# The MLP's up layers one to three as seven products of quarters, with parts of x streamed from DRAM

## The chip, the core and the metric

The kernel runs on one core of one Trainium2 chip. The metric is the device time of one execution, from the first to the last instruction and what lies around them. The core's engines run their own queues of instructions and meet at semaphores: TensorE (PE in the profile, its weight loads PEld), VectorE (DVE), ScalarE (ACT), GpSimd (POOL), and SyncE (SP), which issues transfers.

## What is computed

The kernel is two transformer blocks in a row on 512 tokens of width 1024. The change concerns only the last step of the second block, the MLP:

```python
D_FF = 4 * D_MODEL          # 4096, D_MODEL is 1024, 512 tokens
hm = rmsnorm(x, norm_mlp_g[l])
x = x + jnp.square(jax.nn.relu(hm @ w_up[l])) @ w_down[l]
...
return rmsnorm(x, norm_final_g)
```

## The kernel before

Products of float32 matrices are made from two halves of each operand: a high half, rounded to the format that TensorE takes, and a low half, the rest. `three_pass` (line 229) issues three matmuls, high by high, high by low, low by high. So each weight tile of 128x2048 numbers (1 MB, a "unit") is copied by ScalarE into its high half (`unit_high`, line 2843) and subtracted into its low half by GpSimd or VectorE (`unit_lower`, line 2851; `LOWERED_BY_VECTOR` says which are VectorE's). Units stand in rings of three, so the high half of one waits for the product three before it.

The MLP is cut into four layers of 1024 features. Layer zero's up product (`up0`) is a dense layer like the others in the kernel. In layers one to three an up product (`up`, line 3106) takes eight tiles of 128 features by 512 tokens, eight steps of 128 along the width each, so 64 times three matmuls of 512 columns, with four units. Its result leaves PSUM by `rectified` on VectorE, is squared on ScalarE, and is cut into parts for the down product.

The down product (`down`, line 3136) is already Strassen's in Winograd's form: the two matrices are cut into quarters, seven products of sums of quarters (`product`, line 3120) take the place of eight. The sums of the features are made by `sums` (line 3004) with low halves by `parts_low`, the sums of the weights by `weights_1` to `weights_4`; each product's result is added to the rows of x by `add` (line 3042) on VectorE. Products share PSUM banks: a later one accumulates on the result of an earlier one, and so it waits until that has been added (`p_added`).

Every engine's order is written out by hand in `mlp_sync`, `mlp_gpsimd`, `mlp_scalar`, `mlp_vector` and `mlp_tensor`. An engine stands still at an instruction whose semaphore isn't there yet, with all that is queued behind it.

## Time and profile before

| what | us |
|---|---|
| median of three runs | 1572.93 (1571.53 to 1573.01) |
| profiled execution, its span | 1574.5 |
| TensorE busy | 1550.3 |
| VectorE busy | 980.6 |
| ScalarE busy | 790.5 |
| GpSimd busy | 591.0 |
| the MLP's stages, from up0 to the last product | 1235.4 to 1568.1 of the span |

The profiled execution's own time is its span, with nothing beside it that the profile shows. Busy time of an engine is the time in which at least one of its instructions ran. Matmuls overlap their neighbours, so how long one keeps TensorE is read from the distance of starts. A wait is put down to the instruction that ended it.

### The profile page before, as it was taken

To read this page: it belongs to the slowest core of one execution; us is meant where nothing else is said; L and a number is where in the kernel's file an instruction comes from. 1 tells how busy PE (TensorE), PEld (TensorE's weight loads), DVE (VectorE), ACT (ScalarE), POOL (GpSimd) and SP (SyncE) were. 2 spreads that over 40 slices of the span, in tenths; PEclk is the share of its full clock that TensorE was granted. 3 is DMA by queue.
4 is the path that set the end of the run, shared out by engine and by line. 5 is a ranking of instruction groups with operands and counts; after the bars stand their busy time and mean duration, and the time that the engine had idled before them with its cause. 6 is when DMAs were issued, how large, how long until landed. Compare 5 with 4: busy or idle time off the path is not lost.

```text
span 1574.5 us, 20093 instructions
## 1 busy us (share of the span) xinstructions
PE 1550.3 (98%) x7516; PEld 1263.7 (80%) x7516; DVE 980.6 (62%) x1234; ACT 790.5 (50%) x926; POOL 591.0 (38%) x254
## 2 busy tenths in 40 slices
PE   9999999999999899999999999999999999999998
PEld 7888788687878788888889868767888888888886
DVE  6366211783465699999987479773454574656556
ACT  5265222435245588888875251695334353434344
POOL 1422354533442232232221746444332335252524
PEclk9999999999999999999999999999999999999999
DMA  5421242212237799999976314401420405050411
GB/s 206 128 74 54 80 148 95 106 54 107 82 111 294 276 420 413 386 389 385 390 276 254 116 67 142 131 1 54 160 81 27 161 27 187 28 187 27 171 57 54
DMA packets 50055, 252.18 MB, mean 160 GB/s; under 512 B 9984, under 2 KB 12800, under 8 KB 23744
## 3 DMA queue, kind: packets, MB, share of 16 engines
q1 hardware_dynamic: 43344, 237.89, 41.0%
q0 software_dynamic: 5184, 8.40, 1.5%
q10 hardware_dynamic: 1456, 4.92, 0.8%
q8 instruction: 47, 0.77, 0.2%
q14 instruction: 24, 0.20, 0.0%
HBM read 235.57 MB, written 16.78 MB: 160 GB/s over the span
## 4 chain that ended last, share of the span: by engine, by line
PE 84%; issue 5%; DVE 5%; DMA 2%; ACT 2%; POOL 2%; SPq 0%; ACTq 0%; DVEq 0%; POOLq 0%; PEldq 0%
PE psum L232 23%; PE psum L234 23%; PE psum L233 23%; POOL w_both L148 2%; PE psum L703 2%; PE psum L2402 2%; PE psum L2437 1%; PE psum L1080 1%; PE psum L2425 1%; PE psum L1373 1%; DMA moe_w<-in_w_moe 1%; PE psum L705 1%; PE psum L724 1%; PE psum L2726 1%; PE psum L1059 1%
## 5 line engine op out<-in xcount | busy, mean ns | idle before, releaser
L148 POOL TENSOR_TENSOR w_both<-raw,w_both 128x2048 fp32r<-128x2048 f32 x62 | 288.9, 4659 | 438.0 <-ACT w_both L142 403.1
L1391 DVE TENSOR_TENSOR moe_lo<-moe_w,moe_hi 128x2048 fp32r<-128x2048 f32 x100 | 228.0, 2291 | 35.7 <-ACT moe_hi L1381 34.8
L232 PE MATMUL psum<-x_hi,w_both 128*128 128x512 f32 (+1 forms) x624 | 241.8, 388 | 2.6 <-POOL w_both L148 2.6
L234 PE MATMUL psum<-x_hi,w_both 128*128 128x512 f32 (+1 forms) x624 | 239.5, 384 | 0.0
L233 PE MATMUL psum<-x_lo,w_both 128*128 128x512 f32 (+1 forms) x624 | 239.5, 384 | 0.0
L142 ACT ACTIVATE w_both<-raw 128x2048 fp32r<-128x2048 f32 x67 | 128.0, 1911 | 196.3 <-PE psum L234 194.3
L1381 ACT ACTIVATE moe_hi<-moe_w 128x2048 fp32r<-128x2048 f32 x100 | 191.3, 1915 | 34.3 <-PE psum L234 16.6
L2854 POOL TENSOR_TENSOR unit_lo<-mlp_raw,unit_hi 128x2048 fp32r<-128x2048 f32 x24 | 111.1, 4630 | 180.2 <-ACT unit_hi L2849 102.6
L232 PEld LDWEIGHTS psum<-x_hi,w_both 128*128 128x128 f32 x624 | 117.3, 188 | 27.7 <-issue 3.1
L233 PEld LDWEIGHTS psum<-x_lo,w_both 128*128 128x128 f32 x624 | 117.3, 188 | 23.2 <-issue 0.5
L234 PEld LDWEIGHTS psum<-x_hi,w_both 128*128 128x128 f32 x624 | 117.2, 188 | 23.3
L2849 ACT ACTIVATE unit_hi<-mlp_raw 128x2048 fp32r<-128x2048 f32 x40 | 76.3, 1914 | 77.1 <-PE psum L234 44.6
L232 PE MATMUL psum<-moe_hi,moe_xt_hi 128*128 128x512 f32 x256 | 100.6, 393 | 2.8 <-issue 1.6
L234 PE MATMUL psum<-moe_hi,moe_xt_lo 128*128 128x512 f32 x256 | 99.8, 390 | 0.0
L233 PE MATMUL psum<-moe_lo,moe_xt_hi 128*128 128x512 f32 x256 | 99.7, 389 | 0.0
L232 PE MATMUL psum<-unit_hi,f_hi 128*128 128x512 f32 x224 | 87.5, 391 | 0.9 <-DVE res_rows L3049 0.6
L232 PE MATMUL psum<-y_hi,w_both 128*128 128x512 f32 x224 | 87.8, 392 | 0.0
L234 PE MATMUL psum<-y_hi,w_both 128*128 128x512 f32 x224 | 87.2, 389 | 0.0
L234 PE MATMUL psum<-unit_hi,f_lo 128*128 128x512 f32 x224 | 87.2, 389 | 0.0
L233 PE MATMUL psum<-y_lo,w_both 128*128 128x512 f32 x224 | 87.2, 389 | 0.0
L233 PE MATMUL psum<-unit_lo,f_hi 128*128 128x512 f32 x224 | 87.1, 389 | 0.0
L232 PE MATMUL psum<-x_hi,unit_hi 128*128 128x512 f32 x192 | 74.7, 389 | 0.0
(438 smaller groups left out, 3358.2 us busy)
## 6 DMA issues: line engine op xcount, KB each, us to landing
raw<-in_w_dense SPq DMA_DIRECT2D x67, 1024.0 KB, 4.9
moe_w<-in_w_moe_ahead SPq DMA_DIRECT2D x54, 1024.0 KB, 13.2
moe_w<-in_w_moe SPq DMA_DIRECT2D x48, 1024.0 KB, 13.8
mlp_raw<-in_w_mlp SPq DMA_DIRECT2D x28, 1024.0 KB, 4.9
yrow<-expert_rows SPq DMA_DIRECT2D x8, 512.0 KB, 7.1
res<-in_x SPq DMA_DIRECT2D x4, 512.0 KB, 6.7
decay<-in_decay SPq DMA_DIRECT2D x8, 256.0 KB, 5.2
hn_rows<-hn_tok ACTq DMA_DIRECT2D x4, 512.0 KB, 6.3
```

The source lines that it names most:

```text
L142: act.activation(w_hi[c % RING][:, :], raw[c % RING][:, :], ACT.Copy).then_inc(hi_ready, 1)
L148: pool.tensor_tensor(w_lo[c % RING][:, :], raw[c % RING][:, :], w_hi[c % RING][:, :].bitcast(F32), ALU.subtract).then_inc(lo_ready, 1)
L232: pe.matmul(out, lh, rh, start=first, stop=False, **more)
L233: pe.matmul(out, lh, rl, start=False, stop=False, **more)
L234: return pe.matmul(out, ll, rh, start=False, stop=last, **more)
L703: pe.matmul(psum[:, bank, :], x_hi[:, kt, rows], wb[:, :, :, kt, :], start=kt == 0, stop=kt == KT - 1, skip_group_check=True)
L705: mm = pe.matmul(psum[:, bank, 0:2 * P], x_lo[:, kt, rows], wb[:, 0, :, kt, :], start=False, stop=kt == KT - 1, skip_group_check=True)
L1381: act.activation(ring_hi[s % MOE_HI][:, :], ring[s][:, :], ACT.Copy).then_inc(moe_high, 1)
L1391: dve.tensor_tensor(ring_lo[s][:, :], ring[s][:, :], ring_hi[s % MOE_HI][:, :].bitcast(F32), ALU.subtract).then_inc(moe_low, 1)
L2402: mm = pe.matmul(out, lhs, rhs, start=(qt != 0), stop=True, skip_group_check=True)
L2849: act.activation(unit_hi[(U + 2) % 3][:, :], unit_source(U)[:, :], ACT.Copy).then_inc(highs_done, 1)
L2854: eng.tensor_tensor(unit_lo[(U + 2) % 3][:, :], unit_source(U)[:, :], unit_hi[(U + 2) % 3][:, :].bitcast(F32), ALU.subtract).then_inc(lows ...
```

## The change

In layers one to three the up product becomes seven products too. The weights of the up layer come in quarters (512 of the width by 512 features), the quarters of x (512 of the width by 256 tokens) and their four sums are made once, with high and low halves, and written to DRAM (`x_parts`); each product loads its part back into a ring of three (`x_ring`). A product (`features`) is 48 matmuls of 256 columns. Four of the seven results accumulate in one pair of banks, others are copied by ScalarE (`copy_out`) and added by VectorE (`rectified_quad`), so that the four quarters Q11, Q12, Q22, Q21 of the features come out one after the other. Their sums and halves are now made quarter by quarter (`f_sums`, `part_high`, `part_low`). Up and down stages both have seven units; of an up stage's units VectorE lowers the third and the fifth, of a down stage's the first, GpSimd the others. The order of the down products changes to A11, A12, S1, S4, S2, S3, A22, and with it the order of the additions. Layer zero keeps its dense up product, with another order around it. The core of the diff, with the removed lines mostly left out:

```diff
-        add_residual(dve, "o_cross", norm_mlp)
+        add_residual(dve, "o_cross", norm_mlp, invert=False)
...
-    LOWERED_BY_VECTOR = (0, 2, 3, 5)
-    UNITS = PRODUCTS + 4
+    STAGES = 2 * G - 1
+    PART_OF_PRODUCT = (A11, A12, S1, S4, S2, S3, A22)
+    BANKS_X, BANKS_UP, BANKS_Y, BANKS_Z = (1, 2), (6, 7), (4, 5), (3, 0)
...
+    f_quads = at("f_quads", 112, [P, 2, 2, 4, MIDDLE])
+    Q11, Q12, Q22, Q21 = (1, 0), (1, 1), (0, 1), (0, 0)
+    x_quads = at("x_quads", 188, [P, 2, 2, 4, MIDDLE])
+    x_quads_lo = at("x_quads_lo", 188, [P, 2, 2, 4, MIDDLE], FR)
+    x_quads_hi = at("x_quads_hi", 144, [P, 2, 2, 4, MIDDLE], FR)
+    X_SUMS = ((2, Q22), (5, Q21), (4, Q11), (3, Q12))
+    x_parts = nc.dram_tensor("x_parts", [PRODUCTS, P, 2, 4, MIDDLE], F32).ap()
+    x_ring = [at(f"x_part{b}", 48 + 8 * b, [P, 2, 4, MIDDLE], FR) for b in range(3)]
+    first_s1 = at("first_product", 72, [P, 2, S])
+    c_relu = [at(f"c_relu{h}", 76 + 2 * h, [P, S]) for h in range(2)]
...
+    SUM_OF_UNIT = {2: 1, 4: 2, 5: 3, 6: 4}
+    RAW_OF_UNIT = (B11, B21, B11, B22, B11, B12, B21)
+    LOWERED_BY_VECTOR = ((0,), (2, 4))
...
+        def load_part(K):
+            if K < PRODUCTS * (G - 1):
+                g, n = divmod(K, PRODUCTS)
+                if K >= 3:
+                    before = divmod(K - 3, PRODUCTS)
+                    sp.wait_ge(p_done, 2 * PRODUCTS * (2 * before[0] + 1) + 2 * before[1] + 2)
+                sp.dma_start(x_ring[K % 3][:, :, :, :].bitcast(F32), x_parts[n]).then_inc(part_landed[K % 3], 16)
...
+            part(3)
+            part(4)
+            weights(B11, 3, 3)
+            part(5)
+            weights(B21, 4, 4)
+            part(6)
+            weights(B12, 5, 4)
+            part(7)
+            part(8)
+            weights(B22, 6, 4)
+            part(9)
...
+    def x_sum_low(eng, i, lowered):
+        q = X_SUMS[i][1]
+        eng.wait_ge(xs_high, CROSS + i + 1)
+        if i in (0, 2):
+            eng.wait_ge(xs_added, CROSS + (3, 0, 4)[i])
+        eng.tensor_tensor(quad(x_quads_lo, q), quad(x_quads, q), quad(x_quads_hi, q).bitcast(F32), ALU.subtract)\
+           .then_inc(lowered, 1)
...
+        x_sum_low(pool, 0, xs_low_pool)
+        x_sum_low(pool, 1, xs_low_pool)
...
+        def square(g, q):
+            for h in range(2):
+                act.wait_ge(c_relued, CROSS + quad_count(g, q, h))
+                act.activation(quad(f_quads, q, h), c_relu[h][:, :].rearrange("p (m n) -> p m n", n=MIDDLE), ACT.Square)\
+                   .then_inc(c_squared, 1)
+
+        def part_high(g, part, q):
+            for h in range(2):
+                if part in SUM_COUNT:
+                    act.wait_ge(f_summed, sums_count(g, SUM_COUNT[part]))
+                else:
+                    act.wait_ge(c_squared, SQUARED + quad_count(g, q, h))
+                act.activation(f_parts[h][:, :, 0, part, :], quad(f_quads, q, h), ACT.Copy).then_inc(f_high, 1)
+
+        def copy_out(g, n, h):
+            act.wait_ge(p_done, 2 * PRODUCTS * (2 * g - 1) + 2 * n + h + 1)
+            if n == 3:
+                act.wait_ge(c_squared, SQUARED + quad_count(g, Q11, h))
+            elif n == 1 and g > 1:
+                act.wait_ge(c_squared, SQUARED + quad_count(g - 1, Q21, h))
+            out = first_s1[:, h, :] if n == 2 else c_relu[h][:, :]
+            act.activation(out, psum[:, (BANKS_Z if n == 1 else BANKS_Y)[h], :], ACT.Copy).then_inc(s1_copied, 1)
...
+            up, down = PRODUCTS * (2 * g - 1), PRODUCTS * 2 * g
+            unit_high(act, up + 2)
+            unit_high(act, up + 3)
+            copy_out(g, 1, 0)
+            copy_out(g, 1, 1)
+            unit_high(act, up + 4)
+            copy_out(g, 2, 0)
+            square(g, Q11)
+            copy_out(g, 2, 1)
+            unit_high(act, up + 5)
+            copy_out(g, 3, 0)
+            part_high(g, A11, Q11)
+            copy_out(g, 3, 1)
+            unit_high(act, up + 6)
+            square(g, Q12)
+            unit_high(act, down)
+            part_high(g, A12, Q12)
+            square(g, Q22)
+            unit_high(act, down + 1)
+            part_high(g, A22, Q22)
+            unit_high(act, down + 2)
+            square(g, Q21)
+            part_high(g, S1, Q22)
+            unit_high(act, down + 3)
+            part_high(g, S4, Q12)
+            part_high(g, S2, Q11)
+            part_high(g, S3, Q21)
...
+    SUM_COUNT = {S1: 1, S3: 2, S2: 3, S4: 4}
+    ADDED_AFTER = {0: -13, 1: 0, 2: -9, 3: -10, 4: 3, 5: 2, 6: -8}
+    ADDED_TO = ((2, 0), (2, 0), (0, 1), (2, 1), (2, 1), (0, 1), (0, 0))
...
+        def f_sums(g):
+            q11, q12, q22, q21 = (quad(f_quads, q) for q in (Q11, Q12, Q22, Q21))
+            dve.wait_ge(c_squared, SQUARED + quad_count(g, Q21, 1))
+            dve.tensor_tensor(q22, q21, q22, ALU.add).then_inc(f_summed, 1)
+            dve.tensor_tensor(q21, q11, q21, ALU.subtract).then_inc(f_summed, 1)
+            dve.wait_ge(f_summed, sums_count(g, 1))
+            dve.tensor_tensor(q11, q22, q11, ALU.subtract).then_inc(f_summed, 1)
+            dve.wait_ge(f_summed, sums_count(g, 3))
+            dve.tensor_tensor(q12, q12, q11, ALU.subtract).then_inc(f_summed, 1)
+
+        def part_low(g, part, q):
+            for h in range(2):
+                dve.wait_ge(f_high, part_count(g, part, h))
+                dve.tensor_tensor(f_parts[h][:, :, 1, part, :], quad(f_quads, q, h),
+                                  f_parts[h][:, :, 0, part, :].bitcast(F32), ALU.subtract).then_inc(f_low, 1)
+
+        def rectified_quad(g, q, h):
+            first = 2 * PRODUCTS * (2 * g - 1)
+            n = {Q11: 1, Q12: 4, Q22: 5, Q21: 6}[q]
+            x = psum[:, BANKS_UP[h], :]
+            nth = quad_count(g, q, h)
+            dve.wait_ge(p_done, first + 2 * n + h + 1)
+            if q in (Q22, Q21):
+                dve.wait_ge(c_squared, SQUARED + nth - 2)
+            out = c_relu[h][:, :]
+            if q != Q21:
+                dve.wait_ge(s1_copied, copies_count(g, {Q11: 1, Q12: 3, Q22: 2}[q], h))
+                other = first_s1[:, h, :] if q == Q22 else out
+                dve.tensor_tensor(out, x, other, ALU.add).then_inc(c_read, 1)
+                dve.wait_ge(c_read, READ + 6 * (g - 1) + 2 * C_ORDER.index(q) + h + 1)
+            m = "p (m n) -> p m n"
+            rstd = norm_mlp.rstd[:, MIDDLE * q[0]:MIDDLE * (q[0] + 1)].unsqueeze(1).to_broadcast([P, 2, MIDDLE])
+            ins = dve.scalar_tensor_tensor(out=out.rearrange(m, n=MIDDLE), in0=(x if q == Q21 else out).rearrange(m, n=MIDDLE),
+                                           scalar=0.0, in1=rstd, op0=ALU.max, op1=ALU.mult)
+            ins.then_inc(c_relued, 1)
+
...
+        x_sums()
+        x_sum_low(dve, 2, xs_low_dve)
+        x_sum_low(dve, 3, xs_low_dve)
+        norm_mlp.vector_invert(dve)
         norm_mlp.wait_inverted(dve)
         dve.wait_ge(bank_free, UP0_T + 4)
+        for c in range(4):
+            rectified(2 * c)
+            rectified(2 * c + 1)
+            sums(c)
+            parts_low(c)
+            if c == 2:
+                unit_lower(dve, 0)
+                weights(0, 1)
+        dve.wait_ge(rows_read, ONCE + 2 * TB)
+        add(0, 0)
+        weights(0, 2)
+        weights(0, 3)
+        add(0, 1)
+        weights(0, 4)
+        add(0, 2)
+        add(0, 3)
+        add(0, 4)
+        add(0, 5)
+        for g in range(1, G):
+            up, down = 2 * g - 1, 2 * g
+            add(g - 1, 6)
+            weights(up, 1)
+            unit_lower(dve, PRODUCTS * up + 2)
+            weights(up, 2)
+            weights(up, 3)
+            rectified_quad(g, Q11, 0)
+            rectified_quad(g, Q11, 1)
+            weights(up, 4)
+            unit_lower(dve, PRODUCTS * up + 4)
+            part_low(g, A11, Q11)
+            rectified_quad(g, Q12, 0)
+            rectified_quad(g, Q12, 1)
+            unit_lower(dve, PRODUCTS * down)
+            rectified_quad(g, Q22, 0)
+            part_low(g, A12, Q12)
+            rectified_quad(g, Q22, 1)
+            weights(down, 1)
+            part_low(g, A22, Q22)
+            rectified_quad(g, Q21, 0)
+            rectified_quad(g, Q21, 1)
+            f_sums(g)
+            part_low(g, S1, Q22)
+            weights(down, 2)
+            part_low(g, S4, Q12)
+            add(g, 0)
+            weights(down, 3)
+            part_low(g, S2, Q11)
+            part_low(g, S3, Q21)
+            add(g, 1)
+            add(g, 2)
+            weights(down, 4)
+            add(g, 3)
+            add(g, 4)
+            add(g, 5)
...
+        def features(g, n):
+            L, K = 2 * g - 1, PRODUCTS * (g - 1) + n
+            wh, wl = unit(PRODUCTS * L + n)
+            pe.wait_ge(part_landed[K % 3], PARTS_LANDED[K % 3] + 16 * (K // 3 + 1))
+            x = x_ring[K % 3]
+            banks = (BANKS_UP, BANKS_Z, BANKS_Y, BANKS_Y, BANKS_UP, BANKS_UP, BANKS_UP)[n]
+            for h in range(2):
+                if n == 0 and g > 1:
+                    pe.wait_ge(c_relued, CROSS + quad_count(g - 1, Q21, h))
+                elif n < 3:
+                    pe.wait_ge(p_added, 2 * PRODUCTS * (g - 1) + 2 * (1, 1, 3)[n] + h + 1)
+                elif n == 3:
+                    pe.wait_ge(s1_copied, copies_count(g, 2, h))
+                else:
+                    pe.wait_ge(c_relued, CROSS + quad_count(g, C_ORDER[n - 4], h))
+                for m in (2 * h, 2 * h + 1):
+                    out = psum[:, banks[h], MIDDLE * (m % 2):MIDDLE * (m % 2 + 1)]
+                    for k in range(4):
+                        w = slice(m * P, (m + 1) * P)
+                        mm = three_pass(pe, out, wh[:, k, w], wl[:, k, w], x[:, 0, k, :], x[:, 1, k, :],
+                                        n < 3 and m % 2 == 0 and k == 0, k == 3, skip_group_check=True)
+                mm.then_inc(p_done, 1)
+
...
+        def product(g, n, pairs=range(4)):
+            wh, wl = unit(PRODUCTS * 2 * g + n)
+            f = PART_OF_PRODUCT[n]
             for i in range(2):
+                if n >= 3:
+                    pe.wait_ge(p_added, 2 * PRODUCTS * g + 2 * (2, 0, 4, 5)[n - 3] + i + 1)
+                elif n == 0 and g:
+                    pe.wait_ge(p_added, 2 * PRODUCTS * (g - 1) + 2 * 6 + i + 1)
                 rows = slice(i * P, (i + 1) * P)
                 for c in pairs:
```

## Rows read from the trace of the kernel before

**Rows 1.** The page, part 1: the span, and TensorE's busy time, share, instructions.

```profile
span 1574.5 us, 20093 instructions
PE 1550.3 (98%) x7516; PEld 1263.7 (80%) x7516; DVE 980.6 (62%) x1234; ACT 790.5 (50%) x926; POOL 591.0 (38%) x254
```

**Rows 2.** Busy time by window: layer one's up stage, then its down stage.

```profile
core 0: us, PE busy (x) PEld busy (x) DVE busy (x) ACT busy (x) POOL busy (x), PEclk, DMA share, GB/s
...
1322.40:1365.90 43.50, 43.50 (x193) 36.04 (x192) 20.56 (x25) 16.77 (x14) 13.58 (x4) 1.00 0.22 80
1365.90:1404.30 38.40, 38.31 (x169) 31.44 (x168) 26.98 (x25) 15.54 (x9) 18.76 (x5) 1.00 0.35 128
```

**Rows 3.** Waits of TensorE, 1235.4 to 1574: us in total, times, longest.

```profile
PE psum L232 <- DVE res_rows L3049: 0.6, 1, 0.6
```

**Rows 4.** Timeline of TensorE: first matmul of four stages (start us, us).

```profile
1283.43 0.39 PE L232 MATMUL psum<-unit_hi,f_hi 128*128 128x512 f32 x1
...
1322.39 0.39 PE L232 MATMUL psum<-x_hi,unit_hi 128*128 128x512 f32 x1
...
1365.91 0.39 PE L232 MATMUL psum<-unit_hi,f_hi 128*128 128x512 f32 x1
...
1404.35 0.39 PE L232 MATMUL psum<-x_hi,unit_hi 128*128 128x512 f32 x1
```

**Rows 5.** Timeline of TensorE: matmuls of 256 columns, 46 steps apart.

```profile
836.03 0.28 PE L233 MATMUL psum<-moe_lo,v_mem_in_hi 128*128 128x256 f32 x1
...
841.53 0.28 PE L234 MATMUL psum<-moe_hi,v_mem_in_lo 128*128 128x256 f32 x1
```

**Rows 6.** Timeline of GpSimd: three low halves.

```profile
1238.90 4.61 POOL L148 TENSOR_TENSOR w_both<-raw,w_both 128x2048 fp32r<-128x2048 f32 x1 [7.60 <-ACT w_both L142]
...
1262.41 6.41 POOL L148 TENSOR_TENSOR w_both<-raw,w_both 128x2048 fp32r<-128x2048 f32 x1 [9.37 <-ACT w_both L142]
...
1298.09 4.63 POOL L2854 TENSOR_TENSOR unit_lo<-mlp_raw,unit_hi 128x2048 fp32r<-128x2048 f32 x1 [12.08 <-DVE unit_lo L2854]
```

**Rows 7.** Timeline of VectorE around the same times.

```profile
1237.72 0.69 DVE L396 TENSOR_TENSOR norm_mlp_sum<-norm_mlp_sum,norm_mlp_sq 128x512 f32<-128x512 f32 x1
...
1239.37 4.68 DVE L396 TENSOR_TENSOR norm_mlp_sum<-norm_mlp_sum,norm_mlp_sq 128x512 f32<-128x512 f32 x1 [0.96 <-ACT norm_mlp_sq L369]
...
1248.97 3.35 DVE L400 RECIPROCAL norm_mlp_rstd<-norm_mlp_rms 128x512 f32<-128x512 f32 x1 [4.92 <-ACT norm_mlp_rms L373]
...
1262.05 2.29 DVE L3024 TENSOR_TENSOR mlp_raw<-mlp_raw,mlp_raw 128x2048 f32<-128x2048 f32 x1
...
1291.25 2.28 DVE L2854 TENSOR_TENSOR unit_lo<-mlp_raw,unit_hi 128x2048 fp32r<-128x2048 f32 x1
...
1293.45 2.29 DVE L3030 TENSOR_TENSOR mlp_raw<-mlp_raw,mlp_raw 128x2048 f32<-128x2048 f32 x1
...
1297.86 3.67 DVE L3049 TENSOR_TENSOR res_rows<-res_rows,psum 128x512 f32<-128x512 f32 x6
...
1301.44 3.41 DVE L3034 TENSOR_TENSOR mlp_raw<-mlp_raw,mlp_raw 128x2048 f32<-128x2048 f32 x1
```

**Rows 8.** Groups by form, 1000 to 1574: busy us, mean ns, idle before.

```profile
L2854 POOL TENSOR_TENSOR unit_lo<-mlp_raw,unit_hi 128x2048 fp32r<-128x2048 f32 x24 | 111.1, 4630 | 180.2 <-ACT unit_hi L2849 102.6 <-DVE unit_lo L2854 77.0
...
L2849 ACT ACTIVATE unit_hi<-mlp_raw 128x2048 fp32r<-128x2048 f32 x40 | 76.3, 1914 | 77.1 <-PE psum L234 44.6 <-DVE mlp_raw L3034 29.7 <-DVE mlp_raw L3040 2.0
...
L2854 DVE TENSOR_TENSOR unit_lo<-mlp_raw,unit_hi 128x2048 fp32r<-128x2048 f32 x16 | 36.6, 2286 | 0.6 <-ACT unit_hi L2849 0.6
...
L2917 ACT ACTIVATE f_parts<-f_relu 128x512 f32<-128x512 f32 x32 | 19.7, 632 | 76.8 <-DVE f_relu L3001 76.8
...
L3040 DVE TENSOR_TENSOR mlp_raw<-mlp_raw,mlp_raw 128x2048 f32<-128x2048 f32 x4 | 9.2, 2292 | 0.5
...
L2672 DVE TENSOR_TENSOR cross_score<-cross_score,cinv 128x1024 f32<-128x1024 f32 x4 | 4.9, 1226 | 0.1
```

**Rows 9.** The page, part 6: loads of a unit, us to landing.

```profile
mlp_raw<-in_w_mlp SPq DMA_DIRECT2D x28, 1024.0 KB, 4.9
```

More of the change, by code:

```diff
@@ L2829, in wait_source @@
[L2829 to L2841 removed]
+        L, n = divmod(U, PRODUCTS)
@@ new lines, in mlp_scalar @@
+        for g in range(1, G):
[26 more added lines that the diff above has]
+            part_high(g, S3, Q21)
+            for n in range(2, PRODUCTS):
+                if down + n + 2 < PRODUCTS * STAGES:
+                    unit_high(act, down + n + 2)
```

414 lines of the change are left out of this document (199 added, 215 removed).

## Prediction

> **What bounds the kernel now.** The page's first part comes first: TensorE is busy for 1550.3 of 1574.5 us [rows 1]. The stages of the MLP, one window each, show the same: 43.50 of 43.50 us in an up stage and 38.31 of 38.40 in a down stage, at a granted clock of 1.00, the full 2.4 GHz [rows 2]. TensorE's waits over the whole MLP are a single one of 0.6 us [rows 3]. So this stage is worth what TensorE's instructions cost, as long as the other engines stay ahead; a change that costs TensorE less must be checked against them.
>
> How long a matmul takes is read from starts, not from durations: the durations overlap. From the first matmul of up layer one to the first of its down stage 43.52 us pass for 192 matmuls of 512 columns, 226.7 ns each; the down stage takes 38.44 us for 168, so a layer takes 81.96 us [rows 4]. Matmuls of 256 columns with the same kind of weights start 5.50 us apart over 46 steps, 119.6 ns each [rows 5]. That is more than half of 226.7: the two spacings together give 0.418 ns a column and 12.5 ns for each matmul, and the 12.5 are paid twice as often.
>
> **TensorE's own gain.** An up layer of 192 matmuls of 512 columns becomes 7 products of 48 matmuls of 256: 336 x 0.1196 = 40.2 us for 43.5. The gain is 3.3 us a layer, 10 us over three. The columns alone (86,016 for 98,304, seven eighths) would give 5.4; I take 3.3, since both spacings are measured.
>
> **What the other engines get.** Per layer GpSimd makes the low halves of 11 units (5 of the up stage, 6 of the down stage), for 7 before. At 4.63 us each [rows 8] that is 50.8 us. VectorE gets eight weight sums instead of four and three low halves instead of four, of 2048 columns, 2.20 us apart when back to back (1291.25 to 1293.45 in [rows 7]): 11 x 2.20 = 24.2. It also gets 14 low halves of parts of 512 columns, 0.65 each (0.69 for such an addition alone [rows 7]); four sums of 1024 columns at 1.2 [rows 8]; three quads of two halves, each an addition from PSUM at 0.60 (six take 3.67 [rows 7]) and a rectification whose two inputs are both in SBUF, 0.65; one quad rectified from PSUM; and 14 additions of results at 0.60. Sum: 24.2 + 9.1 + 4.8 + 7.5 + 1.3 + 8.4 = 55 us of some 78 us. ScalarE has 14 high halves at 1.91 and some 28 instructions of 512 columns at 0.6 [rows 8], 44 us. Each engine alone would fit.
>
> Two of them don't fit side by side. An addition on VectorE of 512 columns takes 0.69 alone; started at 1239.37, while GpSimd ran from 1238.90 to 1243.51, it took 4.68 and ended 0.54 after GpSimd. Another of 2048 columns, started at 1301.44, took 3.41 and ended 2.13 after GpSimd's end at 1302.72. The reverse is there too: GpSimd's 4.6 became 6.41 when VectorE had begun a weight sum 0.36 us before it. Six additions from PSUM in the middle of a GpSimd instruction took their usual 3.67 us [rows 6, 7]. So VectorE with both inputs in SBUF and GpSimd take turns, for whole instructions.
>
> The Trainium skill ("SBUF — State Buffer", section "Who interferes with whom") says the same as a rule: a VectorE instruction with two SBUF inputs needs the read port that it shares with GpSimd, and whichever of the two starts second is blocked until the first ends. The trace agrees, with the 4.68 us for 0.69 above; by the rule a layer can't be shorter than the turns' sum, without it the engines would overlap.
>
> The turns of a layer after the change: GpSimd 50.8, sums and low halves of weights 24.2, low halves of parts 9.1, the four sums 4.8, six rectifications 3.9: 92.8 us, for 78.6 us of TensorE (40.2 + 38.4). Before, all of GpSimd and all of VectorE together, PSUM work included, came to 13.6 + 18.8 + 20.6 + 27.0 = 80.0 of 82 us [rows 2]. So 92.8 is the floor of the new layer, if no turn is lost.
>
> **The chain through a layer.** The time t counts from the first matmul of an up stage; a feature product is 5.75 us, a down product 5.46; U and D are units of the up and the down stage. A high half needs the product three before it done; signals between engines cost 0.1 to 0.3. Where GpSimd and VectorE both want a turn I let VectorE go on, since its next instruction is already queued; the rows don't show who wins, and the other case is a rival.
>
> Up: VectorE's first weight sum ends at 3.8, U2 is low at 8.0. Until U4 is low VectorE runs three more weight sums, quad Q11 and U4, while GpSimd takes 4.6 for U3: t = 23.5 to 24.3 for a wish of 23.0, so product 4 is 1 us late. Then GpSimd lowers U5 (to 29.9) and U6 (30.5 to 35.1). Q12's first half is added from PSUM at 27.4, its rectification waits for U5; the second waits for U6 until 35.7. The second half of product 5 begins at 36.0 for 33.7, and ends at 38.9. On VectorE's queue stands `unit_lower` of D0 between Q12 and Q22: square (ScalarE) 36.4, high half 38.3, low half 40.5, then Q22's first half 41.9. Product 6 writes the bank that Q22 is read from, so it starts at 42.1 for 38.9, and the up stage ends at 47.9, not 40.2.
>
> Down: D1 is lowered by GpSimd 47.0 to 51.6, D2 52.9 to 57.5. VectorE's four sums of quads wait for D2 and run to 62.3, S1's low half to 63.5; product 2 can start at 63.2 for 58.8. The costly wait is product 3's: it accumulates into product 2's bank, so it needs `add(g, 2)`, and that stands on VectorE behind weight sum 2, S4's low half (67.0), D3's turn on GpSimd (71.6), weight sum 3, S2, S3 (76.3) and `add(g, 1)` (77.5). Product 2 ended at 68.7, product 3 starts at 78.4: 9.7 us. Four more products end at 100.2. So a layer is 100.2, 18.2 us longer than 82.0.
>
> **Layer zero.** Ahead of it ScalarE scales x eight times (4.8 us) and makes four high halves of 1024 columns (about 4, half of 1.91 each) from about 1239.4, where the last square was done; split, root and reciprocal, which began at 1248.97 [rows 7], come some 5 us later. The transposes in TensorE's queue wait for the root: 2 us; the rest hides behind tiles two and three. The loads of x (7 MB a layer, beside 8 MB of weights) are needed two products after their slot is free, 11 us for 4.9 [rows 9]: hidden, and without that cover 5 us each. In SP's queue they stand ahead of loads of weights; the latest, B22 of the down stage, waits behind the part that product 5 frees (38.9) and lands by 45, for D3's high half at 60. At the end of up0 unit 1's high half now stands behind VectorE's low halves, `unit_lower(0)`, the weight sum and two rectifications: done 1291.7, low half 1296.3, while products 0's first three quarters end 1289.9: 6.5 us. Product 3 waits for `add(0, 2)` behind three weight sums and U3's turn: another 6.6. With 2 at the start that is 15 us for layer zero.
>
> Sum on the profiled execution: 1574.5 + 15 + 3 x 18.2 = 1644. That execution lies 1.6 us above the runs' median of 1572.9, so 1643 to compare with the median.
>
> **Rivals.**
> - No turns cost: if the two engines overlapped, or the order happened to keep them apart, the same chain gives a wait of 1.5 us for Q22 and 4 us for product 3, some 84.6 a layer (+2.6), and +11 in layer zero: 1592. For it: GpSimd's mean of 4.63 before is hardly above its 4.62 alone [rows 6, 8]. Against it: the rows on turns. 0.19.
> - GpSimd goes first whenever it waits: part lows get one turn per GpSimd instruction, the S1 low half comes at 69.8 and product 3 at 89.5; a layer takes 111, layer zero 18 more: 1574.5 + 18 + 87 - 1.6 = 1678. Nothing in the rows speaks for or against. 0.15.
> - Faster: TensorE stays the bound, as it is in [rows 3]. Then 3 x 3.3 comes off: 1563. It needs `add(g, 2)` no later than product 2's end, that is VectorE 10 us earlier in the down stage than above, 4 even without turns. 0.08. It decides at a wait of 3.3 us a layer; above that the change loses.
> - No difference: waits of just 3.3 us a layer. 0.03.
>
> The chain as worked out has 0.55; its own range is 1625 to 1665 (half or one and a half of product 3's wait). For 8 in 10 the range takes in the first two rivals: 1588 to 1682. Faster (by over 0.2%, about what a measurement here can tell) 0.08, same 0.03, slower 0.89. What the granted clock does after waits of 5 to 10 us isn't shown by these rows; a fall would come on top and lies within the upper end.
>
> **What would show it.** Right: feature matmuls 120 ns apart in runs; TensorE's waits in layers one to three led by `res_rows` additions, at 70 to 90 us into a layer; VectorE's 512-column instructions of 2 to 5 us; GpSimd low halves over 4.7. Layers of 95 to 105 us. Wrong: layers of 80 with no such wait, or feature matmuls further apart than 120 ns, which would make TensorE itself slower (each 10 ns costs 3.4 us a layer), or waits led by DMA, if the parts of x come late.

## The result and the profile after

| | median us | range | ratio to before |
|---|---|---|---|
| before | 1572.23 | 1571.53 to 1573.01 | |
| after | 1677.24 | 1674.28 to 1679.06 | 1.0661 [1.0646, 1.0676] |

The changed kernel is 6.6% slower; 1643 (1588 to 1682) was predicted, so the time lies inside the range and near its upper end. The change was forecast to cost 70 us and costs 105. The page of the changed kernel, part 1, with span, busy time, share and instructions of each engine:

```profile
span 1677.2 us, 21150 instructions
PE 1570.9 (94%) x7948; PEld 1298.0 (77%) x7948; DVE 1114.7 (66%) x1258; ACT 828.1 (49%) x995; POOL 679.6 (41%) x271
```

TensorE was busy for 98% [rows 1] and is now for 94%; no other engine is near its limit over the whole span. The waits of TensorE from 1235 us to the end (us in total, times, longest):

```profile
PE psum L232 <- DVE f_parts L3163: 29.3, 3, 9.9
PE psum L232 <- issue: 27.1, 4, 8.3
PE psum L232 <- DVE c_relu L3182: 13.9, 3, 4.6
PE psum L232 <- DVE res_rows L3216: 10.0, 1, 10.0
PE psum L232 <- POOL unit_lo L2863: 3.3, 1, 3.3
```

One wait of 0.6 us [rows 3] has become 85 us of waits, nearly all for VectorE. The first three lines are waits of each layer from one to three: before down product 2, before down product 3 (the fourth is at the end of up0), before up product 5; products are counted from 0. No DMA stands in the list. Where they fall shows in TensorE's timeline, first matmuls in layer two: the up stage, the down stage, down products 2 and 3, and the next up stage:

```profile
1452.90 0.28 PE L232 MATMUL psum<-x_part,unit_hi 128*128 128x256 f32 x1
...
1500.95 0.40 PE L232 MATMUL psum<-unit_hi,f_parts 128*128 128x512 f32 x1
...
1521.76 0.77 PE L232 MATMUL psum<-unit_hi,f_parts 128*128 128x512 f32 x1 [9.74 <-DVE f_parts L3163]
...
1537.51 0.77 PE L232 MATMUL psum<-unit_hi,f_parts 128*128 128x512 f32 x1 [8.10 <-issue]
...
1561.90 0.28 PE L232 MATMUL psum<-x_part,unit_hi 128*128 128x256 f32 x1
```

A layer takes 1561.90 - 1452.90 = 109.0 us, for 81.96 before [rows 4] and 100.2 predicted. The same layer in windows, the up stage and then the down stage, and six short stretches of the granted clock (after down product 2's start, after product 3's, the next 4 us, the start of layer zero's down stage, the start of its product 3, and the start of up product 5 in layer two):

```profile
core 0: us, PE busy (x) PEld busy (x) DVE busy (x) ACT busy (x) POOL busy (x), PEclk, DMA share, GB/s
1452.90:1501.00 48.10, 42.98 (x338) 42.40 (x337) 42.30 (x26) 23.02 (x25) 18.90 (x5) 0.93 0.56 211
1501.00:1561.90 60.90, 43.05 (x169) 34.62 (x169) 45.25 (x32) 18.90 (x17) 34.97 (x8) 0.83 0.25 93
1521.80:1525.30 3.50, 3.50 (x8) 2.74 (x9) 3.50 (x4) 0.79 (x1) 0.00 (x0) 0.50 0.00 0
1537.50:1541.00 3.50, 3.49 (x8) 2.79 (x9) 3.50 (x2) 0.00 (x0) 2.51 (x1) 0.50 0.00 0
1541.00:1545.00 4.00, 4.00 (x15) 3.20 (x14) 1.85 (x2) 0.00 (x0) 0.00 (x0) 0.75 0.46 131
1284.20:1291.00 6.80, 6.80 (x17) 5.34 (x18) 5.02 (x7) 3.89 (x4) 0.85 (x1) 0.55 0.94 392
1320.10:1324.50 4.40, 4.40 (x11) 3.47 (x12) 0.41 (x1) 0.00 (x0) 3.64 (x1) 0.50 0.70 238
1487.40:1491.80 4.40, 4.32 (x20) 4.35 (x21) 1.87 (x3) 3.70 (x5) 0.00 (x0) 0.50 0.26 110
```

VectorE is now counted busy for 42.30 + 45.25 = 87.6 us of a layer, for 20.56 + 26.98 = 47.5 before [rows 2]. Much of that is waiting inside an instruction. The clock is the second thing to see: after the two long waits of the down stage it is 0.50, the lower level of 1.2 GHz, and the same 3.5 us hold 8 matmuls instead of 15. It is 0.50 behind the wait of up product 5 too, where 20 matmuls of 256 columns start 0.21 us apart instead of 0.12: 2.0 us.

What VectorE did before product 2 and product 3, in its timeline:

```profile
1500.33 9.71 DVE L3163 TENSOR_TENSOR f_parts<-f_quads,f_parts 128x512 fp32r<-128x512 f32 x2 [0.82 <-ACT f_parts L3006]
1509.96 1.28 DVE L3182 SCALAR_TENSOR_TENSOR c_relu<-psum,norm_mlp_rstd 128x512 f32<-128x512 f32 x2
...
1516.61 5.61 DVE L3163 TENSOR_TENSOR f_parts<-f_quads,f_parts 128x512 fp32r<-128x512 f32 x2
...
1526.74 6.46 DVE L3200 TENSOR_TENSOR mlp_raw<-mlp_raw,mlp_raw 128x2048 f32<-128x2048 f32 x1
1533.13 2.48 DVE L3163 TENSOR_TENSOR f_parts<-f_quads,f_parts 128x512 fp32r<-128x512 f32 x4
1535.54 2.47 DVE L3216 TENSOR_TENSOR res_rows<-res_rows,psum 128x512 f32<-128x512 f32 x4
```

and GpSimd's timeline beside it:

```profile
1499.86 9.63 POOL L2863 TENSOR_TENSOR unit_lo<-mlp_raw,unit_hi 128x2048 fp32r<-128x2048 f32 x2 [13.07 <-ACT unit_hi L2858]
1516.22 4.85 POOL L2863 TENSOR_TENSOR unit_lo<-mlp_raw,unit_hi 128x2048 fp32r<-128x2048 f32 x1 [6.73 <-ACT unit_hi L2858]
1526.50 4.56 POOL L2863 TENSOR_TENSOR unit_lo<-mlp_raw,unit_hi 128x2048 fp32r<-128x2048 f32 x1 [5.43 <-ACT unit_hi L2858]
```

Two low halves of A22, 1.28 us when nothing stands in their way, took 9.71. GpSimd had two low halves queued, the first from 1499.86; they took 9.63, that is twice 4.6 and one short instruction between them. The ends fit one reading alone: GpSimd's first, VectorE's first, GpSimd's second (to 1509.49), VectorE's second (to 1510.04). At 1516.61 GpSimd had one instruction, and VectorE lost one turn; the weight sum at 1526.74 lost one too (6.46 for 2.28). The wait called "issue" before product 3 ends with the additions that start at 1535.54, as `add(g, 2)` is the second pair of these four.

### The profile page after: what moved, and what is told of

Same layout as the page of the kernel before. It is cut to its first block, busy times and chain, and to the rows that moved or that the text cites. A ratio compares the mean times of both kernels' runs of the same rounds, so it can differ in the third digit from the quotient of the medians.

```text
span 1677.2 us, 21150 instructions
## 1 busy us (share of the span) xinstructions
PE 1570.9 (94%) x7948; PEld 1298.0 (77%) x7948; DVE 1114.7 (66%) x1258; ACT 828.1 (49%) x995; POOL 679.6 (41%) x271
## 4 chain that ended last, share of the span: by engine, by line
PE 66%; DVE 13%; issue 10%; ACT 4%; DMA 3%; POOL 3%; SPq 1%; ACTq 0%; DVEq 0%; POOLq 0%; PEldq 0%
PE psum L232 17%; PE psum L234 17%; PE psum L233 17%; DVE f_parts L3163 3%; POOL w_both L148 2%; PE psum L703 2%; ACT unit_hi L2858 2%; PE psum L2402 1%; DVE mlp_raw L3200 1%; PE psum L2437 1%; POOL unit_lo L2863 1%; DVE unit_lo L2863 1%; PE psum L1080 1%; PE psum L2425 1%; PE psum L1373 1%
## 5 line engine op out<-in xcount | busy, mean ns | idle before, releaser
L2863 POOL TENSOR_TENSOR unit_lo<-mlp_raw,unit_hi 128x2048 fp32r<-128x2048 f32 x39 | 194.8, 4994 | 197.6 <-ACT unit_hi L2858 167.9
L232 PE MATMUL psum<-unit_hi,f_parts 128*128 128x512 f32 x224 | 97.5, 435 | 69.8 <-DVE f_parts L3163 29.3
L2858 ACT ACTIVATE unit_hi<-mlp_raw 128x2048 fp32r<-128x2048 f32 x49 | 93.6, 1910 | 138.8 <-PE psum L234 77.8
L232 PE MATMUL psum<-x_part,unit_hi 128*128 128x256 f32 x336 | 98.6, 294 | 15.3 <-DVE c_relu L3182 13.9
L232 PEld LDWEIGHTS psum<-unit_hi,f_parts 128*128 128x128 f32 x224 | 47.6, 212 | 83.7 <-issue 39.1
L232 PE MATMUL psum<-moe_hi,moe_xt_hi 128*128 128x512 f32 x256 | 100.4, 392 | 1.6 <-issue 1.6
L233 PE MATMUL psum<-x_part,unit_hi 128*128 128x256 f32 x336 | 97.6, 290 | 0.0
L234 PE MATMUL psum<-x_part,unit_lo 128*128 128x256 f32 x336 | 97.3, 290 | 0.0
L233 PE MATMUL psum<-unit_lo,f_parts 128*128 128x512 f32 x224 | 95.3, 425 | 0.0
L234 PE MATMUL psum<-unit_hi,f_parts 128*128 128x512 f32 x224 | 94.7, 423 | 0.0
```

What stands on the lines that cost most here:

```text
L232: pe.matmul(out, lh, rh, start=first, stop=False, **more)
L233: pe.matmul(out, lh, rl, start=False, stop=False, **more)
L234: return pe.matmul(out, ll, rh, start=False, stop=last, **more)
L2858: act.activation(unit_hi[(U + 2) % 3][:, :], unit_source(U)[:, :], ACT.Copy).then_inc(highs_done, 1)
L2863: eng.tensor_tensor(unit_lo[(U + 2) % 3][:, :], unit_source(U)[:, :], unit_hi[(U + 2) % 3][:, :].bitcast(F32), ALU.subtract).then_inc(lows ...
```

## The experiments

The theory: VectorE's instructions with both inputs in SBUF and GpSimd's subtractions take turns for whole instructions, VectorE is late by that, and TensorE waits at three places a layer. Rivals: GpSimd's own duration sets the chain; the order of VectorE's queue does it without any turns; the clock does it; the amount of VectorE's work does it. Each time is compared with the kernel before on the same chip in the same job (medians of 1572.8 to 1573.3). The runs in which GpSimd only writes or reads one operand leave the low halves of GpSimd's units out of the result; all others compute the whole. Waits in the text below are distances between the starts on either side of a gap, some 0.3 us more than the idle time in the lists of waits.

| run | us | ratio | a layer, us |
|---|---|---|---|
| GpSimd only writes | 1600.33 | 1.0167 [1.015, 1.0185] | 86.0 to 87.5 |
| additions first | 1664.07 | 1.0579 [1.0561, 1.0597] | 103.6 to 105.1 |
| four low halves to VectorE | 1655.94 | 1.0526 [1.0508, 1.0543] | 100.4 to 102.0 |
| fill before products 2 and 3 | 1675.36 | 1.0646 [1.0625, 1.0667] | 108.2 to 109.3 |
| GpSimd only writes, longer | 1601.67 | 1.0183 [1.0157, 1.0209] | 86.2 to 87.7 |
| that, additions first | 1586.83 | 1.0086 [1.0069, 1.0102] | 80.6 to 81.9 |
| both edits, six low halves to VectorE | 1629.92 | 1.0353 [1.0336, 1.037] | 91.3 to 93.9 |
| longer fill | 1673.07 | 1.0636 [1.0618, 1.0654] | 107.1 to 107.3 |
| layer zero reordered too | 1622.74 | 1.0314 [1.0295, 1.0334] | 93.2 to 93.7 |
| all low halves on VectorE | 1631.8 | 1.0374 [1.0356, 1.0391] | 95.1 to 95.3 |
| GpSimd reads one operand | 1616.17 | 1.0272 [1.0254, 1.029] | 90.2 to 91.9 |
| up stages' on VectorE | 1620.47 | 1.0292 [1.0268, 1.0317] | 89.9 to 92.4 |

**GpSimd only writes.**

```diff
-                unit_lower(pool, U)
+                unit_zeroed(pool, U)
...
+        for i in range(32):
+            ins = pool.memset(low[:, 64 * i:64 * i + 64], 0.0)
+        ins.then_inc(lows_done, 1)
```

> GpSimd's low halves of the MLP's units are replaced by 32 small fills with zero, about as long in all, which write and read nothing; the low halves of those units are left out of the result. Theory (VectorE instructions with two inputs in SBUF take turns with GpSimd's subtractions): no VectorE instruction is stretched any more, the waits before product 6 of the up stage and before down products 2 and 3 shrink to about 1.5, 2 and 4 us, a layer takes 84 to 90 us for 109, the whole 1595 to 1625 us. Rival (VectorE is late from its own load and order alone, whatever GpSimd does): layers stay at 105 or more, the whole above 1660.

Measured 1600.33, with 86.0 to 87.5 us a layer: down product 2's wait is gone and so is up product 5's (4.9 before), up product 6 now waits 2.2, and down product 3's wait falls from 8.4 to 4.1. But the fills took 2.84 us a unit (110.7 us for 39) where the subtraction takes 4.6, so shorter work on GpSimd could have done the same. Hence the longer fill below.

**Additions first.** `add(g, 1)` and `add(g, 2)` ahead of the third weight sum.

```diff
             add(g, 0)
+            add(g, 1)
+            add(g, 2)
             weights(down, 3)
             part_low(g, S2, Q11)
             part_low(g, S3, Q21)
-            add(g, 1)
-            add(g, 2)
             weights(down, 4)
```

> Only VectorE's order changes: the additions of results 1 and 2 stand ahead of the third weight sum and of the low halves of S2 and S3. Theory (down product 3 waits for addition 2, which stands in VectorE's queue behind a weight sum that waits for GpSimd): product 3's wait of 8.3 us goes to under 1.5; some 3 us come back at product 6, whose unit now is low later; a layer is 5 to 8 us shorter, the whole 1652 to 1664 us. Rival (the wait, which the trace puts down to nothing it shows, is for the unit's low half or for something else): no change, 1674 to 1680.

13 us less. Product 3's wait of 8.4 us is gone, as forecast; down product 2's and up product 5's are as they were (10.0 and 4.9). A new wait of 3.8 to 4.7 us stands before down product 5, for `add(g, 4)`. VectorE's timeline in layer two, and TensorE's first matmul of product 5:

```profile
1529.65 6.69 DVE L3204 TENSOR_TENSOR mlp_raw<-mlp_raw,mlp_raw 128x2048 f32<-128x2048 f32 x1
1536.26 2.47 DVE L3216 TENSOR_TENSOR res_rows<-res_rows,psum 128x512 f32<-128x512 f32 x4
...
1538.23 0.77 PE L232 MATMUL psum<-unit_hi,f_parts 128*128 128x512 f32 x1 [3.74 <-issue]
```

The fourth weight sum took 6.69 us for 2.28, a lost turn, and `add(g, 4)` is the second pair of the four additions behind it. So the queue's order holds product 3, as the prediction's chain had it, and about half of what its wait cost came back at product 5, not at product 6 as the expectation had it.

**Four low halves to VectorE** (up units 5 and 6, down units 1 and 2).

```diff
-    LOWERED_BY_VECTOR = ((0,), (2, 4))
+    LOWERED_BY_VECTOR = ((0, 1, 2), (2, 4, 5, 6))
...
+            unit_lower(dve, PRODUCTS * up + 5)
...
+            unit_lower(dve, PRODUCTS * up + 6)
...
+            unit_lower(dve, PRODUCTS * down + 1)
...
+            unit_lower(dve, PRODUCTS * down + 2)
```

> In layers one to three the low halves of up units 5 and 6 and of down units 1 and 2 move from GpSimd to VectorE (2.2 us each there for 4.6). Theory of turns: the sum of turns falls by 9.7 us a layer, product 2's wait from 10 to 2 to 5 us, product 5's from 4.6 to 1 to 2; a layer is 5 to 9 us shorter, the whole 1648 to 1662 us. Rival (VectorE's own load): VectorE gets 8.8 us more a layer, the whole is 1690 to 1705 us.

More work on VectorE, and 21 us less: a low half costs VectorE 2.29 us itself and over 4.6 when it waits behind GpSimd's. Down product 2's wait falls from 10 to 4.9; up product 5's (4.9) is gone, and up product 6 waits 3.2 instead; down product 3's, which stands behind other turns, stays at 8.0 to 8.8.

**Fill before products 2 and 3**: 70 and 58 added matmuls of 256 columns on banks that are free at that time, so that TensorE isn't idle.

```diff
+            if g and n == 2:
+                pe.wait_ge(s1_copied, copies_count(g, 3, 1))
+                filler(BANKS_Y, 70)
+            if g and n == 3:
+                pe.wait_ge(c_relued, CROSS + quad_count(g, Q21, 1))
+                filler(BANKS_UP, 58)
```

> TensorE gets matmuls that nobody reads (70 of 256 columns before down product 2, 58 before product 3, in layers one to three) to run in its two long waits. After each such wait the granted clock is 0.50 for 3.5 us and more in the changed kernel's trace. Theory: the low clock follows from the wait, and it costs only where TensorE then sets the pace, after product 3's wait: 2.4 us a layer; after product 2's the next wait swallows it. The clock stays at 1.00 through the down stages and the whole is 1668 to 1672 us. Rivals: every slow stretch costs (4 us a layer, 1663 to 1667), or the clock falls for another reason (1676 to 1680).

1675.36, above the expectation. Windows of this run, layer two: product 2, the idle rest of product 3's wait, product 3's start:

```profile
1519.30:1524.90 5.60, 5.60 (x25) 4.64 (x26) 5.60 (x7) 1.92 (x1) 0.78 (x1) 1.00 0.01 3
1532.00:1535.10 3.10, 0.00 (x0) 0.00 (x0) 3.10 (x7) 0.89 (x1) 2.13 (x1) 0.82 0.81 312
1535.10:1538.60 3.50, 3.46 (x8) 2.79 (x9) 3.50 (x2) 0.00 (x0) 2.61 (x1) 0.50 0.01 5
```

Product 2 runs at 1.00 here, but what that gives only lengthens product 3's wait; the second fill ended 3.1 us too early, and the clock fell to 0.50 all the same. So this run didn't test what it was made for.

**GpSimd only writes, longer**: 53 pieces a unit instead of 32.

```diff
-        for i in range(32):
-            ins = pool.memset(low[:, 64 * i:64 * i + 64], 0.0)
+        for i in range(52):
+            ins = pool.memset(low[:, 39 * i:39 * i + 39], 0.0)
+        ins = pool.memset(low[:, 39 * 52:], 0.0)
```

> As the first run (GpSimd only writes: a fill with zeros in place of each of its low halves, which leaves those halves out), but the fill cut into 53 pieces instead of 32, so that GpSimd is busy for about as long a unit (4 to 5 us) as the subtraction was; the first run's fills took only 2.84 us. Theory (what costs VectorE its time is that GpSimd reads two SBUF operands, not that GpSimd is busy that long): 1598 to 1612 us, at most 4 us a layer above the first run's 86.1, because only the last low halves before a product land later. Rival (the chain waits for GpSimd's own duration): most of the 109 us a layer is back, 1640 us or more.

1601.67, the same within the intervals as with the shorter fill. VectorE's low halves of parts and GpSimd's work from 1340 to 1560 us, by groups (busy us, mean ns, idle before), of this run:

```profile
L3172 DVE TENSOR_TENSOR f_parts<-f_quads,f_parts 128x512 fp32r<-128x512 f32 x36 | 23.0, 685 | 9.9 <-ACT f_parts L3015 9.9
...
L2871 POOL MEMSET unit_lo<- 128x39 f32 x1431 | 96.0, 131 | 129.8 <-ACT unit_hi L2858 129.7
```

and the same group in the changed kernel, same stretch:

```profile
L3163 DVE TENSOR_TENSOR f_parts<-f_quads,f_parts 128x512 fp32r<-128x512 f32 x28 | 52.2, 1908 | 1.6 <-ACT f_parts L3006 1.6
```

0.685 us each for 1.908, with not one instruction stretched. GpSimd was busy for 96.0 us over 27 units here, 3.6 each. That is 0.7 more a unit than with the shorter fill, though still not the subtraction's 4.6, and none of it came back in the time. Each piece is only 0.13 us long, so a lost turn would be short here; but not even that shows: in layers one to three, the 24 low halves of parts that ran beside pieces took 0.686 us on the mean and at most 0.693, the 18 with GpSimd idle 0.683. So it isn't to GpSimd's writes that VectorE loses its time; whether reads or length do it is settled by the copy below.

**That, additions first**: the last kernel with the edit of the second run.

> The longer fills of the run above (GpSimd's low halves left out) and the additions of down products 1 and 2 moved ahead of the third sum of weights, as in the second run. Theory: without GpSimd's two-operand reads product 3's gap in the down stage (4.1 us in the first run) was the place of add(g, 2) in VectorE's queue alone, so it falls under 1.5 us: 4 us a layer less than the run above, 1585 to 1600 us; a layer is then 82 to 84 us, level with the kernel before (82.0) and not under it, since TensorE's own 3.3 us a layer go into product 5's gap of some 2 us and the handover between the stages. Rival (Strassen's up stage would win once VectorE is free): under 1571 us, a layer under 81 us.

TensorE's timeline of this run, the starts of two up stages and of their down stages:

```profile
1332.07 0.28 PE L232 MATMUL psum<-x_part,unit_hi 128*128 128x256 f32 x1
...
1374.57 0.40 PE L232 MATMUL psum<-unit_hi,f_parts 128*128 128x512 f32 x1
...
1412.67 0.28 PE L232 MATMUL psum<-x_part,unit_hi 128*128 128x256 f32 x1
...
1455.17 0.40 PE L232 MATMUL psum<-unit_hi,f_parts 128*128 128x512 f32 x1
```

The up stage takes 42.50 us and the down stage 38.10 [rows 4 had 43.52 and 38.44]: 80.6 us a layer, twice, and 81.9 in layer three, where the clock was 0.96. Product 3's gap is gone; the only wait left is the 2.2 us of up product 6 (the expectation calls it product 5's), which needs quad Q22 rectified. With no reads by GpSimd, layers one to three come to 243.1 us for 245.7 before, to the last product's last matmul: the seven products give back 2.6 us in three layers, without the low halves. The whole is still slower, because layer zero's down stage takes 49.65 us for 38.96. The rival's "under 1571 us" fell; its layer of under 81 us was there in two layers of three.

**Both edits, six low halves to VectorE** (the second and the third run's edits, and down units 3 and 4 on VectorE).

```diff
-    LOWERED_BY_VECTOR = ((0, 1, 2), (2, 4, 5, 6))
+    LOWERED_BY_VECTOR = ((0, 1, 2, 3, 4), (2, 4, 5, 6))
...
+            unit_lower(dve, PRODUCTS * down + 3)
             add(g, 0)
             add(g, 1)
             add(g, 2)
+            unit_lower(dve, PRODUCTS * down + 4)
             weights(down, 3)
```

> The whole computation. The second and third runs' edits together, and the low halves of down units 3 and 4 on VectorE too: VectorE makes 9 of the 14 a layer, GpSimd 5. If the gains add up, 13 and 21 us fall from 1677 and two more units a layer at some 1.7 us each take another 10: 1633 us, 1625 to 1648. Theory of turns: not under the kernel before, since VectorE's own work is 56.2 us a layer with 3 low halves on it and no reads beside it, 70 us with 9, and five GpSimd units at 4.6 us stand between its instructions: about 93 us a layer and 1605 at the very best. Rival (with fewer turns the change wins): under 1570 us.

1629.92: gains at different waits add up, 47 us in all of the 105 lost.

**Longer fill**: 92 matmuls before product 3 instead of 58.

```diff
-                filler(BANKS_UP, 58)
+                filler(BANKS_UP, 92)
```

> The whole computation, with the added matmuls of the fourth run (70 before down product 2) and 92 instead of 58 before product 3, so that TensorE is idle for under 1 us before either. Theory (the clock's fall is a real but small term): the granted clock stays at 1.00 across both restarts, products 3 to 6 run at 227 ns a matmul, a layer ends 2.2 to 2.6 us earlier than after, 1667 to 1671 us. Rival (what the clock gives is taken up by the next wait wherever it is): 1674 to 1678 us.

Windows of this run, product 2 and the first 9.6 us from product 3's start:

```profile
1518.80:1524.30 5.50, 5.50 (x24) 4.56 (x25) 5.50 (x7) 1.92 (x1) 0.72 (x1) 1.00 0.00 0
1535.40:1541.00 5.60, 5.60 (x26) 4.64 (x26) 4.59 (x2) 0.00 (x0) 1.84 (x1) 1.00 0.12 18
1541.00:1545.00 4.00, 4.00 (x19) 3.30 (x19) 1.37 (x2) 1.92 (x1) 2.00 (x1) 1.00 0.95 387
```

The clock stays at 1.00, and products 3 to 6 take 21.8 us for 24.4 after: the clock costs 2.6 us a layer. Some of it is lost again: the fill was a little too long now, and product 3 starts 85.5 us into layer two instead of 84.6. A layer is 107.1 to 107.3. The time, 1673.07, lies 4.2 us under the changed kernel's and between the two expectations; the intervals of the two ratios overlap, so the 2.6 us rest on the windows and not on the whole time.

**Layer zero reordered too.**

```diff
         add(0, 0)
         weights(0, 2)
+        add(0, 1)
+        add(0, 2)
         weights(0, 3)
-        add(0, 1)
         weights(0, 4)
-        add(0, 2)
         add(0, 3)
```

> The whole computation: the run with all three edits, and in layer zero the additions of products 1 and 2 ahead of the third and fourth sums of weights. Theory (layer zero's 24 us are the same thing, add(0, 2) behind two sums that take turns with GpSimd): the 10.4 us gap before its product 3 falls to 2 to 4 us, with one to two us more from the clock: 1620 to 1625 us, layers one to three unchanged at 93.9 us each. Rival (layer zero waits for the low halves of its units on GpSimd): 1628 to 1632 us.

Layer zero's down stage goes from 59.8 to 50.1 us, its 10.4 us gap to 1.0. The whole falls by 7.2.

**All low halves on VectorE**, from the last kernel. GpSimd reads nothing in layers one to three.

```diff
-    LOWERED_BY_VECTOR = ((0, 1, 2, 3, 4), (2, 4, 5, 6))
+    LOWERED_BY_VECTOR = (tuple(range(PRODUCTS)), tuple(range(PRODUCTS)))
...
+            unit_lower(dve, PRODUCTS * up + 3)
...
+            unit_lower(dve, PRODUCTS * down + 5)
...
+            unit_lower(dve, PRODUCTS * down + 6)
...
+                unit_lower(dve, PRODUCTS * (down + 1))
...
+                unit_lower(dve, PRODUCTS * (down + 1) + 1)
```

> The whole computation, as the run above with all 14 low halves of layers one to three on VectorE, so that GpSimd reads nothing there. VectorE's own work is then 56.2 + 11 x 2.28 = 81.2 us a layer. Theory of turns (a low half on GpSimd costs VectorE more than making it): every VectorE instruction runs at its own time, 0.69 us for a part's half and 2.28 for a sum, and a layer takes 84 to 91 us, 1592 to 1614 us in all: less than any other whole version, and still not under the kernel before, whose layer is 82.0. Rival (VectorE's amount of work is what binds, shared or not): a layer stays at 94 us or grows, 1622 us or more.

Every duration is as the theory had it: 0.686 us a part's half, 2.286 to 2.289 a sum. The time is the rival's: 95.1 to 95.3 us a layer. Windows of this run, layer one's down stage and layer two's up stage, and TensorE's waits from 1340 to 1560 us:

```profile
1382.20:1432.70 50.50, 41.98 (x170) 33.53 (x169) 42.15 (x39) 18.74 (x17) 0.00 (x0) 0.93 0.29 105
1432.80:1477.40 44.60, 41.98 (x337) 41.81 (x336) 37.96 (x30) 23.34 (x25) 0.00 (x0) 0.96 0.62 236
```

```profile
PE psum L232 <- DVE unit_lo L2865: 9.8, 2, 4.9
PE psum L232 <- issue: 6.9, 2, 3.4
PE psum L232 <- DVE c_relu L3184: 5.2, 2, 2.6
```

VectorE works for 80.1 of 95.1 us and is late all the same: in the down stage 42.15 of 50.5 us, where product 5 waits 5.3 us. The list names a low half, the one of unit 6 that ended last before the matmul; unit 5's own was done at 1411.88. What product 5 needed was `add(g, 4)`, and that stands in VectorE's queue behind unit 6's low half (the expectation of the last run below has this wait wrong too). VectorE's timeline, and TensorE's first matmul of product 5:

```profile
1417.31 2.29 DVE L2865 TENSOR_TENSOR unit_lo<-mlp_raw,unit_hi 128x2048 fp32r<-128x2048 f32 x1 [0.84 <-ACT unit_hi L2860]
1419.52 1.28 DVE L3218 TENSOR_TENSOR res_rows<-res_rows,psum 128x512 f32<-128x512 f32 x2
...
1420.30 0.77 PE L232 MATMUL psum<-unit_hi,f_parts 128*128 128x512 f32 x1 [4.91 <-DVE unit_lo L2865]
```

So turns are what the changed kernel loses by, and without them the amount of work on VectorE, in this order, is enough to be late.

**GpSimd reads one operand**: a copy in place of the subtraction.

```diff
-                unit_lower(pool, U)
+                unit_copied(pool, U)
...
+        pool.tensor_copy(unit_lo[(U + 2) % 3][:, :], unit_source(U)[:, :]).then_inc(lows_done, 1)
```

> The changed kernel with GpSimd's subtraction replaced by a copy of the weights (it reads one operand in SBUF instead of two and writes as much; the low halves of its units are left out and the raw values stand there). Theory (two-operand reads of both engines take turns; one-operand reads do not): VectorE's halves of parts run at 0.69 us and the time is that of the runs that only wrote, 1598 to 1612 us. Rival (any read by GpSimd from SBUF makes VectorE wait): halves of parts well over 1 us, 1640 us or more.

Neither: 1616.17. VectorE's low halves of parts and GpSimd's copies, by groups, 1340 to 1560 us:

```profile
L3168 DVE TENSOR_TENSOR f_parts<-f_quads,f_parts 128x512 fp32r<-128x512 f32 x33 | 31.8, 1007 | 4.9 <-ACT f_parts L3011 4.9
...
L2869 POOL CAST unit_lo<-mlp_raw 128x2048 fp32r<-128x2048 f32 x26 | 55.4, 2132 | 171.4 <-ACT unit_hi L2858 143.1 <-DVE unit_lo L2863 28.3
```

The mean of 1.007 us, well above 0.685, says that VectorE waits for a copy with one read as well; the turn only lasts 2.1 us instead of 4.6. GpSimd's length is not the cause: the copies are shorter than the fills (3.6 us a unit in the longer ones), and the run is 14 us slower. My theory's "two-operand reads of both" falls; a read by GpSimd is enough. The Trainium skill ("SBUF — State Buffer", section "Who interferes with whom") has it so: a VectorE instruction with two SBUF inputs contends with a GpSimd instruction that reads SBUF, not with one that only writes. The runs agree on both halves, 1.007 us beside copies and 0.685 beside fills.

**Up stages' on VectorE**: as all on VectorE, but down units 5 and 6 on GpSimd.

```diff
-    LOWERED_BY_VECTOR = (tuple(range(PRODUCTS)), tuple(range(PRODUCTS)))
+    LOWERED_BY_VECTOR = ((0, 1, 2, 3, 4), tuple(range(PRODUCTS)))
...
-            unit_lower(dve, PRODUCTS * down + 5)
...
-            unit_lower(dve, PRODUCTS * down + 6)
```

> The whole computation, between the last two whole versions: all seven low halves of the up stages on VectorE (44.65 us an up stage in the run with all on VectorE, 47.1 to 48.4 with two on it late), of the down stages five on VectorE and units 5 and 6 on GpSimd (45.3 to 46.4 us a down stage there, 50.5 with all on VectorE, where product 5 waited 5.3 us for its low half). Theory (the time is set by where VectorE's queue is late, and each stage keeps the better of its two values): a layer takes 90 to 91 us, 1608 to 1620 us in all, the fastest whole version and still some 40 us behind the kernel before. Rival (the work moved to VectorE in the up stage comes back in the down stage): a layer of 93 to 95 us, 1622 to 1632.

1620.47, the fastest whole version; its interval and that of the layer-zero run overlap. The up stages keep their 44.6 us; the down stages take 47.8, 47.8 and 45.2, with 2.4 us of a new wait before product 6 where they were slow. Its own low half was done 3.1 us earlier, at 1421.46 in layer one; it waited for `add(g, 5)` (1423.77 to 1424.45, product 6 at 1424.55), which stands behind the low half of the next up stage's first unit, and that one behind GpSimd's last. So some of the gain came back in the down stage, as the rival had it, and the layer of 92.4 lies between the two.

## Why the prediction was right, and where it was mis-sized

**TensorE's own gain** held: features are 120 ns apart, and without waits the up stage's 336 matmuls take 42.50 - 2.2 = 40.3 us for the 40.2 of the sum.

**Turns** held as the cause: by the durations above, and by 1600 us when GpSimd doesn't read. The rival without turns was well sized (84.6 us a layer; measured 86.0 to 87.5, with waits of 2.2 us for Q22 and 4.1 for product 3, forecast 1.5 and 4).

**The chain through the up stage** ended at 48.05 us in layer two, 47.9 forecast, and this agreement is partly luck. Forecast were 2.3 us before product 5's second half, behind U6, and 3.2 before product 6, for Q22. Measured were 4.8 us lost before product 5's first half and none before product 6. The low half of A11 had waited for U5 (VectorE's pair from 1476.70 took 5.72 us) and Q12's first rectification for U6 (4.28 us from 1483.06): two turns ahead of that first half, where the forecast gave one. The slow clock behind that wait added 2.0 us, which the forecast had at nothing.

**The step that was mis-sized is "I let VectorE go on".** The two engines alternate: a waiting GpSimd instruction gets in between two of VectorE's that stand back to back, and the other way round. A22's two low halves are the plainest case. So product 2 starts at 68.9 us into the layer, not 63.2: +5.7. The rival "GpSimd goes first" was nearer here, in number (69.8, and 1678 in all) and in rule: "one turn per GpSimd instruction" is what alternating gives a chain of short instructions, and the runs don't tell the two apart. It missed at product 3, which started at 84.6 and not at 89.5. That the time lies in the range is owed to this rival, for which the range was stretched to 1682: the chain's own range, 1625 to 1665, did not hold.

**Product 3's wait** was the forecast one, `add(g, 2)` behind sums and turns, at 8.4 us for 9.7; the second run moved it.

**The clock** was left out of the centre and allowed for at the upper end: 2.6 us a layer after product 3 (the longer fill), 1.8 in product 2 that product 3's wait takes up, beside the 2.0 in the up stage. The layer's excess of 8.8 us over 100.2 is then 5.7 at product 2, +1.8 -1.3 for product 2's length and product 3's wait, and 2.6 of clock.

**Layer zero** was 24.3 us longer for 15, counted from the start of up0 to that of layer one. Its waits are 3.2 at the end of up0 (VectorE's `unit_lower(0)`; I had 2, at the start), 3.7 for unit 1 (6.5) and 10.4 before product 3 (6.6): 17.3. What is left, 7 us, is the clock: 37 of the down stage's 168 matmuls start 0.43 us apart or more instead of 0.227, behind each of the three waits, 7.8 us in all (0.55 and 0.50 in the windows above). No run of its own changed the clock alone there.

Sum: 1574.5 + 24.3 + 3 x 27.0, less 2.7 that this execution was ahead when up0 began, is 1677.1; the span is 1677.2. Of the 33 us between the forecast's 1644 and this, turns at product 2 are 17 and the clock some 15, in layer zero and behind product 3. Two small slips of the prediction don't move it: 11 x 4.63 is 50.9 and not 50.8, and its 1.6 us sets a span against times that lie 1.8 to 1.9 us above their spans (1679.06 for 1677.2 here); the forecast is a difference and stays.

Still open is whether some order of VectorE's queue makes the whole change faster than before. The runs show that TensorE's part allows 80.6 us a layer, and that four orders with the low halves made come to 90 to 95.

## What to carry to other kernels

Before moving work off the busiest engine, add up what the others get in turns, not in busy time: VectorE's instructions with two SBUF inputs and GpSimd's reading ones exclude each other, and 55 us and 51 us "of 78" were two loads that did not fit beside each other. Giving GpSimd's subtractions back to VectorE at 2.3 us each was worth more than 4.6 us on an engine that seemed free. A 3.3 us gain of TensorE's is gone with the first wait of that length, and in the changed kernel each wait of 2.8 us and more had a slow stretch of the clock behind it.
